# A two-block transformer kernel: bias rows made in the context's tail, a third buffer for modulation weights, and shift and scale columns turned on TensorE from SBUF

## The chip, the cores and the metric

The kernel runs on one core of a Trainium2 chip. The metric is device time in microseconds (us), the median of several executions; the profile is of one execution of its own.

## What is computed

Two blocks run one after the other on 256 tokens of width 1024. The first (two layers) is a hybrid mixer (retention, a block attention whose scores get a relative bias from a small table, a short convolution) and a convolutional feed-forward part. The second (two layers) attends from the tokens to themselves and to a context of 256 tokens, and ends each layer in a PEER mixture: every token picks 128 of 16384 experts, and for each pick a row `u` and a row `v` of 1024 values are fetched. Shift, scale and gate of every norm come from a condition vector by the modulation matrices:

```python
for l in range(DEPTH):
    last = l == DEPTH - 1
    sh1, s1, g1, sh2, s2, g2 = jnp.split((sc @ w_mod[l] + b_mod[l])[:, None, :], 6, axis=-1)
    csh1, cs1, cg1, csh2, cs2, cg2 = jnp.split(sc_ctx @ w_mod[l] + b_mod[l], 6, axis=-1)
    hc = modulate(h_ctx, csh1, cs1)
    ...
def modulate(x, shift, scale):
    return rms(x) * (1 + scale) + shift
...
    b_own = rel_t[:, t5_bucket(dist_own)]
    s_own = jnp.einsum('bhqd,bhld->bhql', qi, k_own) * scale + b_own[None]
```

The context's own path (norm, modulation, projection, attention, PEER) doesn't depend on the first block, so the kernel does it first.

## The kernel before, in words

There are three parts, one after the other on every engine: the context (the second block's first layer on the context tokens), the first block ("first", two layers), and the latent part (the second block on the tokens, two layers). Each engine runs its own instruction list, in the order in which the code is written; semaphores tie them together. All direct loads are issued by SyncE (SP) in its order, a few by ScalarE (ACT); the fetches of expert rows (128 rows of 4 KB each) are issued by GpSimd (POOL). The fetches of the context's PEER run beside the first block: ten row buffers, eight in `ROWS` and two in `ACC`, each fetched again when VectorE (DVE) has used it (`beside_used`).

**Modulations.** There are twelve, g = 0 to 11, six for each layer; each is a product of two columns with a 1024x1024 matrix of 4 MiB, 64 matmul records and 8 for the bias row (`mod_pe`, L445 and L448), a copy by ScalarE (`mod_act`, L459) and two stores to `mod_dram`. g = 0 and 1 (shift and scale of the context's first norm) are wanted first; 2 to 5 stand inside the context's projections and mixer; 6 to 11 behind its PEER queries. The matrices of g = 3 to 11 go by turns into the lower half (slots 0, 1) and the upper half (slots 2, 3) of the weight buffer `W`; those of 0 to 2 go in four pieces of 1 MiB into other buffers. One row `MODB` holds the bias of the next modulation.

**Setup.** TensorE makes six rows of relative bias over distance (L1636), ScalarE stores them to `rel_dram` (L1674), and twelve loads issued by ScalarE (L1682) bring them back as overlapping windows `HANK`. TensorE does modulation 0, waits for all twelve, reverses them by six products with `flip` (L1644), and then does modulation 1. ScalarE stores the six bias tiles to `bias_dram`, and brings shift and scale back from `mod_dram` as 16 rows `MODR` (`mod_rows`, L347), which TensorE turns into columns `MODC` (L543). ScalarE applies them while it copies the turned context into `XT` (L928); then the projections start (L322).

**The tail of the context.** While DVE searches the best experts of both token tiles, the loads and products of modulations 6 to 11 run. SyncE's order there is: load g after modulation g - 2 (for g = 7: after the last queries, which read slots 2 and 3), bias row g after modulation g - 1. Behind the last come the first weights of the first block and its input `X`.

**The handover.** The semaphores of the first block's first layer were used by the setup, so GpSimd clears them (`clear_layer(pool, 0)`) and raises `cleared`; TensorE, SyncE, ScalarE and DVE wait for it before the first block. In the kernel before, GpSimd does this in the middle of the context's mixer.

Of the kernel before, what the change touches and what calls it, by code (L numbers as in the profile page):

```python
# [23 lines left out]
ALU = mybir.AluOpType  # L24
# [3 lines left out]
P = 128  # L28
# [68 lines left out]
MOD_SETUP, MOD_FIRST = 2, 3  # L97
# [85 lines left out]
def program(nc, A, out):  # L183
    with ExitStack() as ctx:
# [21 lines left out]
        act_step = sem("act_step")  # L206
        mod_read = sem("mod_read")
        mod_loaded = [sem(f"mod_loaded{i}") for i in range(2)]
# [199 lines left out]

        def mod_piece(g, j):

            if g < MOD_FIRST:
                return PIECES[min(g, 1)][j].rearrange("p (k n) -> p k n", k=DK)
            half = W[:, 2 * (g % 2):2 * (g % 2) + 2, :].rearrange("p s n -> p (s n)").rearrange("p (j k n) -> p j k n", j=MODP, k=DK)
            return half[:, j]
# [4 lines left out]
        def mod_landed(g):  # L419
            return mod_loaded[1 if g == MOD_SETUP else g % 2]  # L420

        def mod_load(sp, g):
            l, i = divmod(g, MODS_N)
            n = P * D * D // P
            src = A["w_mod_2"][l, i * n:(i + 1) * n].rearrange("(p j k n) -> p j k n", p=P, j=MODP, k=DK)
            if g < MOD_FIRST:
                for j in range(MODP):
                    sp.dma_start(mod_piece(g, j), src[:, j]).then_inc(mod_landed(g), 16)
            else:
                half = W[:, 2 * (g % 2):2 * (g % 2) + 2, :].rearrange("p s n -> p (s n)").rearrange("p (j k n) -> p j k n", j=MODP, k=DK)  # L430
                sp.dma_start(half, src).then_inc(mod_landed(g), 16)
# [5 lines left out]
        def mod_pe(pe, s, banks, groups, g):  # L437
            pe.wait_ge(mod_landed(g), 16 * sum(MODP if i < MOD_FIRST else 1 for i in range(g + 1) if mod_landed(i) is mod_landed(g)))
# [98 lines left out]
        def stream_pe_cols(pe, s, banks, groups, stage):  # L537

            pe.wait_ge(small_loaded, 16 * 5 * (stage + 1))
# [1066 lines left out]
        with ExitStack() as ph:  # L1606
# [6 lines left out]
            PIECES = [[AR[:, 0:2 * D], AR[:, 2 * D:4 * D], AR[:, 4 * D:6 * D], BC["QKT"][:]], [AR[:, 6 * D:8 * D], HF, KV[:], ACCF]]  # L1613
            QRF, VF, EIF = (BC[name][:].rearrange("p t n -> p (t n)") for name in ("QR", "V", "EI"))
# [6 lines left out]
            HANK = [BC["PROJ2"][:, h * NB:(h + 1) * NB] for h in range(4)] + [QRF[:, h * NB:(h + 1) * NB] for h in range(2)]  # L1621
# [84 lines left out]
            def context_pe(pe):  # L1706
# [13 lines left out]
                for g in range(MOD_FIRST + 3, L * MODS_N):  # L1720
                    mod_pe(pe, s, banks, groups, g)
# [1167 lines left out]
```

## Time and profile before

| | |
|---|---|
| median of 3 runs | 3053.81 us (3052.48 to 3056.08) |
| profiled execution: its time, its span | 3025.97 us, 3024.2 us |
| mean granted TensorE clock, share of full | 0.897 |
| TensorE, VectorE, ScalarE, GpSimd busy | 2483.7, 2114.5, 831.5, 1115.7 us |
| moved by DMA | 1038.89 MB, mean 344 GB/s |
| chain of waits: DMA, VectorE, TensorE | 31%, 29%, 26% |

Busy shares are means over stages with different limits; the chain of waits tells which one ends last at each moment. The profiled execution took 27.8 us less than the median of the runs.

### The profile page before, as it was taken

To read this page: it belongs to the slowest core of one execution; us is meant where nothing else is said; L and a number is where in the kernel's file an instruction comes from. 1 tells how busy PE (TensorE), PEld (TensorE's weight loads), DVE (VectorE), ACT (ScalarE), POOL (GpSimd) and SP (SyncE) were. 2 spreads that over 40 slices of the span, in tenths; PEclk is the share of its full clock that TensorE was granted. 3 is DMA by queue.
4 is the path that set the end of the run, shared out by engine and by line. 5 is a ranking of instruction groups with operands and counts; after the bars stand their busy time and mean duration, and the time that the engine had idled before them with its cause. 6 is when DMAs were issued, how large, how long until landed. Compare 5 with 4: busy or idle time off the path is not lost.

```text
span 3024.2 us, 27795 instructions
## 1 busy us (share of the span) xinstructions
PE 2483.7 (82%) x8607; PEld 1401.7 (46%) x8607; DVE 2114.5 (70%) x4458; ACT 831.5 (27%) x2284; POOL 1115.7 (37%) x1121
## 2 busy tenths in 40 slices
PE   2997698878898899889788778778798798778776
PEld 1655355655546566555444333323365344333322
DVE  0359769878788988777587677755374776777654
ACT  1131111100012100023443333334324343433343
POOL 0200245666553676460133334333210333333332
PEclk7898796999997999987999889989998899898999
DMA  8255999999999999970499899999830999999998
GB/s 323 112 195 232 388 415 361 384 410 408 403 396 369 398 409 413 390 288 6 173 402 413 360 420 419 417 413 396 329 116 4 366 418 366 420 420 416 418 420 337
DMA packets 182646, 1038.89 MB, mean 344 GB/s; under 512 B 26891, under 2 KB 28914, under 8 KB 99812
## 3 DMA queue, kind: packets, MB, share of 16 engines
q0 software_dynamic: 147456, 805.37, 66.1%
q1 hardware_dynamic: 32700, 229.20, 18.9%
q10 hardware_dynamic: 2344, 2.55, 0.2%
q8 instruction: 70, 1.15, 0.2%
q14 instruction: 76, 0.62, 0.1%
HBM read 1032.61 MB, written 4.44 MB: 343 GB/s over the span
## 4 chain that ended last, share of the span: by engine, by line
DMA 31%; DVE 29%; PE 26%; issue 6%; POOL 4%; ACT 4%; ACTq 0%; SPq 0%; DVEq 0%; POOLq 0%
DMA W<-in_peer_uv,IDX 14%; PE PS L2581 12%; DMA ROWS<-in_peer_uv,IDX 7%; PE PS L322 7%; DVE ROWS L1326 3%; DMA ROWS<-in_peer_uv,COEF 3%; DVE ROWS L2212 3%; POOL ROWS L2412 3%; DVE W L2712 2%; DMA ROWS<-in_peer_uv,IDXV 2%; DVE PROD L2225 2%; PE PS L2013 1%; DVE BJ L1523 1%; DMA G<-in_peer_uv,IDX 1%; PE PS L2023 1%
## 5 line engine op out<-in xcount | busy, mean ns | idle before, releaser
L2581 PE MATMUL PS<-W,SCALE 128*128 128x512 f32 x1712 | 841.5, 639 | 220.7 <-ACT SCALE L2665 220.2
L2712 DVE CUSTOM_DVE_ANT_0 W<-W,PS 128x1024 f32<-128x1024 f32 x428 | 515.2, 1219 | 331.6 <-DMA W<-in_peer_uv,IDX 330.3
L2765 POOL DMA_INDIRECT W<-in_peer_uv,IDX x428 | 407.8, 953 | 687.9 <-PE PS L2581 668.6
L2581 PEld LDWEIGHTS PS<-W,SCALE 128*128 128x128 f32 x1712 | 331.2, 203 | 707.8 <-issue 706.2
L2412 POOL DMA_INDIRECT ROWS<-in_peer_uv,IDX x206 | 216.4, 1050 | 396.2 <-DVE IDX L1587 201.0
L2013 PE MATMUL PS<-XT,W 128*128 128x256 f32 x1408 | 307.8, 380 | 0.0
L2013 PEld LDWEIGHTS PS<-XT,W 128*128 128x128 f32 x1408 | 268.4, 191 | 46.1 <-issue 10.7
L2658 ACT ACTIVATE DOT<-DOT 128x1 f32<-128x1 f32 x512 | 103.6, 202 | 652.7 <-DVE DOT L2712 646.3
L322 PE MATMUL PS<-W,XT 128*128 128x512 f32 (+2 forms) x576 | 220.6, 545 | 10.7 <-ACT XT L928 5.7
L322 PE MATMUL PS<-XT,W 128*128 128x128 f32 (+1 forms) x1344 | 215.4, 320 | 5.7 <-ACT XT L1039 5.7
L2665 ACT ACTIVATE SCALE<-C,COEF 128x128 f32<-128x128 f32 x512 | 205.6, 402 | 48.1 <-PE PS L2581 1.5
L2212 DVE CUSTOM_DVE_ANT_0 ROWS<-ROWS,PS 128x1024 f32<-128x1024 f32 x154 | 182.4, 1216 | 47.3 <-DMA ROWS<-in_peer_uv,IDX 45.5
L322 PEld LDWEIGHTS PS<-XT,W 128*128 128x128 f32 x1344 | 198.0, 191 | 28.5 <-issue 6.7
L322 PEld LDWEIGHTS PS<-W,XT 128*128 128x128 f32 x576 | 108.9, 199 | 120.0 <-issue 108.9
L2661 ACT ACTIVATE COEF<-DOT,WGT 128x1 f32<-128x1 f32 x512 | 150.8, 295 | 48.3 <-ACT DOT L2658 0.7
L322 PE MATMUL PS<-W,CT 128*128 128x512 f32 x320 | 150.2, 629 | 5.2 <-ACT CT L1090 2.5
L2225 DVE SCALAR_TENSOR_TENSOR PROD<-ROWS,COEF,PROD 128x1024 f32<-128x1024 f32 x102 | 131.0, 1284 | 31.4 <-DMA ROWS<-in_peer_uv,COEF 22.2
L2412 POOL DMA_INDIRECT ROWS<-in_peer_uv,COEF x102 | 112.1, 1099 | 57.2 <-DVE PROD L2225 30.9
L2225 DVE SCALAR_TENSOR_TENSOR H<-ROWS,COEF,H 128x1024 f32<-128x1024 f32 x81 | 104.0, 1284 | 27.8 <-DMA ROWS<-in_peer_uv,IDXV 21.5
L2023 PE MATMUL PS<-W,PP 128*128 128x512 f32 x192 | 94.2, 648 | 27.8 <-DVE PP L2380 27.8
L2412 POOL DMA_INDIRECT ROWS<-in_peer_uv,IDXV x82 | 96.1, 1172 | 55.9 <-DVE H L2225 35.8
L1326 DVE SCALAR_TENSOR_TENSOR ROWS<-ROWS,COLC 128x256 f32<-128x256 f32 x270 | 115.1, 481 | 2.3
(386 smaller groups left out, 3141.9 us busy)
## 6 DMA issues: line engine op xcount, KB each, us to landing
W<-in_w_up SPq DMA_DIRECT2D x44, 1024.0 KB, 11.9
W<-in_w_in SPq DMA_DIRECT2D x21, 2048.0 KB, 11.3
W<-in_w_mod SPq DMA_DIRECT2D x9, 4096.0 KB, 14.4
W<-in_w_down SPq DMA_DIRECT2D x22, 1024.0 KB, 8.0
W<-in_w_o SPq DMA_DIRECT2D x6, 2048.0 KB, 9.5
W<-in_peer_wq SPq DMA_DIRECT2D x6, 2048.0 KB, 10.9
W<-in_w_out SPq DMA_DIRECT2D x4, 2048.0 KB, 12.4
W<-in_peer_uv,IDX POOLq DMA_INDIRECT x428, 12.8
```

Of the source, the lines that this page charges most:

```text
L322: ins = nc.tensor.matmul(PS[:, b, cols[0]:cols[1]], lhs(k), rhs(k), start=start and k == 0, stop=stop and k == n_k - 1)
L1326: ins = nc.vector.scalar_tensor_tensor(B["U"][:, j, :], B["PAD"][:, j, k:k + S], tap, B["U"][:, j, :], ALU.mult, ALU.add)
L2013: ins = nc.tensor.matmul(PS[:, 2 * r + half, j * S:(j + 1) * S], up_half(i, half)[:, k, j * P:(j + 1) * P], XT[:, k, :], start=(k == 0), s ...
L2023: ins = nc.tensor.matmul(PS[:, 4 + 2 * t + n, :], HG[r][:, j, t * P:(t + 1) * P], wslot(2 + r, 2, D)[:, j, n * 512:(n + 1) * 512], start=F ...
L2212: nc.vector.tensor_tensor_reduce(beside_slot(l, m), beside_slot(l, m), h, 1.0, 0.0, ALU.mult, ALU.add, DOT[:, 0, m:m + 1]).then_inc(beside ...
L2225: nc.vector.scalar_tensor_tensor(total, slot, coef, total, ALU.mult, ALU.add).then_inc(beside_used, 1)
L2412: nc.gpsimd.indirect_dma_start(beside_slot(l, n), None, one_by_one, bass.IndirectOffsetOnAxis(index[:, n % PICKS:n % PICKS + 1], 0),).then ...
L2581: ins = nc.tensor.matmul(PS[:, SUMS2[t] + h, :], SCALE[:, n % NSCALE, :], v_of(n)[:, h * 512:(h + 1) * 512], start=m == 0, stop=m == PICKS ...
L2661: nc.scalar.activation(COEF[:, t, one], DOT[:, t, one], ACT.Copy, scale=WGT[:, t, one]).then_inc(s.coef_ready, 1)
L2665: nc.scalar.activation(SCALE[:, n % NSCALE, :], ident, ACT.Copy, scale=COEF[:, t, one]).then_inc(s.scale_ready, 1)
L2712: nc.vector.tensor_tensor_reduce(u_of(n), u_of(n), h_of(t), 1.0, 0.0, ALU.mult, ALU.add, DOT[:, t, m:m + 1]).then_inc(s.rows_used, 1)
L2765: nc.gpsimd.indirect_dma_start(pair_slot(n), None, in_pairs, bass.IndirectOffsetOnAxis(IDX[:, t, m:m + 1], 0),).then_inc(pair_landed[fetch ...
```

## The change

- The twelve loads of the bias windows, the six products with `flip` and the stores to `bias_dram` move from the setup into the tail, behind modulation 7. SyncE issues the loads; the windows and the bias tiles lie in `ROWS` and `V`.
- Shift and scale of the context's first norm: TensorE turns `MODS` (the copy of modulations 0 and 1 in SBUF) by four transposes, and DVE takes the wanted columns from PSUM; the way through `mod_dram` stays for the rows that are wanted later.
- Modulation buffers: a third home `TAIL` (the buffers `CT`, `QKT`, `ACC`, `XT`) for g = 7 and 10; modulation 2 gets a semaphore of its own. Loads are issued one modulation earlier relative to their use.
- `clear_layer(pool, 0)` moves from the context's mixer to GpSimd's place between the fetch of row 9 and that of row 10, and waits for `X`.

```diff
+MOD_SETUP, MOD_BESIDE = 2, 6
+FRONT, SECOND, LOWER, UPPER, TAIL = range(5)
+MOD_HOME = [FRONT, SECOND, SECOND, UPPER, LOWER, UPPER, LOWER, TAIL, UPPER, LOWER, TAIL, UPPER]
...
+            PIECES = {FRONT: [AR[:, 0:2 * D], AR[:, 2 * D:4 * D], AR[:, 4 * D:6 * D], BC["QKT"][:]],
+                      SECOND: [AR[:, 6 * D:8 * D], HF, KV[:], ACCF], TAIL: [CTF, BC["QKT"][:], ACCF, XTF]}
...
                 pe.wait_ge(s.cols_ready, 1)
-                mod_pe(pe, s, banks, groups, 0)
+                for g in range(MOD_SETUP):
+                    mod_pe(pe, s, banks, groups, g)
+
+            def bias_pe(pe, banks):
+                s, groups = layers[0], of_setup
                 pe.wait_ge(s.late_rows_loaded, 12 * 16)
                 for h in range(MOBA_H):
                     b = banks.take(s.score_read, h + 1)
                     nc.tensor.matmul(PS[:, b, 0:NB], flip, HANK[h], start=True, stop=True).then_inc(s.groups_done, groups.mark("bias", h))
                     groups.at["bias", h, "bank"] = b
-                mod_pe(pe, s, banks, groups, 1)
...
+            def context_pe_cols(pe, banks):
+                s, groups = layers[1], of_context
+                pe.wait_ge(small_loaded, 16 * 4)
+                b = banks.take(s.cols_ready, 1)
+                for j in range(CW2 // P):
+                    ins = nc.tensor.transpose(PS[:, b, j * 34:j * 34 + 34], COLR[:, j * P:(j + 1) * P], ident[0:34, 0:34])
+                ins.then_inc(s.groups_done, groups.mark("cols"))
+                groups.at["cols", "bank"] = b
+                b = banks.take(s.cols_ready, 1)
+                for g in range(MOD_SETUP):
+                    pe.wait_ge(mod_read, g + 1)
+                    for half in range(2):
+                        o = (2 * g + half) * P
+                        ins = nc.tensor.transpose(PS[:, b, o:o + P], MODS[:, g, half * P:(half + 1) * P], ident)
+                ins.then_inc(s.groups_done, groups.mark("modT"))
...
                 stream_sp(sp, s, groups, BC, 0, 1, beside, first=1)
                 sp.wait_ge(s.groups_done, groups.of("mix", 1, TT - 1))
-                mod_load(sp, MOD_FIRST + 3)
+                mod_load(sp, 6)
+                for j in range(2):
+                    mod_load_piece(sp, 7, j)
...
+                sp.wait_ge(s.h_ready, TT)
+                mod_load_piece(sp, 7, 2)
+                sp.wait_ge(s.groups_done, groups.of("pq", TT - 1, 1))
+                mod_load_piece(sp, 7, 3)
+                mod_load(sp, 8)
+                sp.wait_ge(s.groups_done, groups.of("ps", TT - 1, 1, 1))
+                sp.wait_ge(layers[0].stored, 16)
+                bias_sp(sp)
+                for g in range(7, L * MODS_N):
                     sp.wait_ge(s.groups_done, groups.of("mod", g - 1))
                     mod_bias(sp, g)
-                for c in (0, 1):
-                    first_load(sp, c, 0)
+                    if g + 2 < L * MODS_N:
+                        mod_load(sp, g + 2)
+                    elif g + 2 == L * MODS_N:
+                        for c in (0, 1):
+                            first_load(sp, c, 0)
+                sp.wait_ge(layers[0].stored, 3 * 16)
...
-                pool.wait_ge(s.probs_ready, 1)
-                pool.wait_ge(s.max_ready, 1)
-                pool.wait_ge(s.weights_loaded[2], 16)
-                clear_layer(pool, 0)
...
+                        if l == 0 and n == 6:
+                            pool.wait_ge(layers[0].stored, 3 * 16)
+                        if l == 0 and n == RING:
+                            pool.wait_ge(layers[1].groups_done, of_context.of("mod", 10))
+                        if l == 0 and n == BESIDE:
+                            pool.wait_ge(x_loaded, 16)
+                            clear_layer(pool, 0)
```

How the instructions stand shows what the diff alone leaves open. First ScalarE's list in the setup before, from its copy of the bias over distance (`V`) to the first activation that makes `XT`; `mod_dram<-X` are the stores of a modulation.

```order
L1674 DMA rel_dram<-V 6x511 [waits act_step]
...
L1682 DMA QR<-rel_dram 128x256
L459 COPY X<-PS 128x256 [waits groups_done_0]
L463 DMA mod_dram<-X 4x256 [waits mod_read]
L463 DMA mod_dram<-X 4x256
L1686 COPY QKT<-PS 128x384 [waits groups_done_0] x5
L1686 COPY QR<-PS 128x384 [waits groups_done_0]
L459 COPY X<-PS 128x256 [waits groups_done_0]
...
L347 DMA G<-mod_dram 16x128 [waits mod_stored1,mod_stored0]
L1691 DMA bias_dram<-QKT 128x1920 [waits score_read_0]
L1692 DMA bias_dram<-QR 128x384
L928 ACTIVATE XT<-PS,MODC 128x128 [waits groups_done_1,cols_ready_1]
```

Twelve loads, six copies, the load of `MODR` and two stores stand between modulation 0's place and the first activation there. In the changed kernel the same stretch of TensorE's list, from the bias row of modulation 1 (`ROW`) to the first projection, reads as follows; `G` holds the small rows, `X` is `MODS`.

```order
L456 MATMUL PS<-ROW,ONE 32x256 x4
L561 MATMUL PS<-C,CT 128x128 [waits norm_ready_1]
L561 MATMUL PS<-C,CT 128x128 x7
L561 MATMUL PS<-C,CT 128x128 [waits cols_ready_0,norm_ready_1]
L561 MATMUL PS<-C,CT 128x128 x3
L561 MATMUL PS<-C,CT 128x128 [waits proj_ready_0]
L561 MATMUL PS<-C,CT 128x128 x3
L1725 MATMUL PS<-C,G 128x34 [waits mod_read,small_loaded]
L1725 MATMUL PS<-C,G 128x34 x3
L1733 MATMUL PS<-C,X 128x128 [waits mod_read]
...
L323 MATMUL PS<-W,XT 128x512 [waits xT_ready_1,first_loaded0]
```

The sixteen transposes of the context stand behind modulation 1 in both kernels; what follows them now waits for ScalarE's copy of modulation 1 alone. Last, GpSimd's list of the changed kernel from the first fetch to row 10; the `ISA` row is the clearing, `x_loaded` the load of `X` behind all modulations.

```order
L2471 DMA ROWS<-in_peer_uv,IDX 128x1024 [waits picks_ready_1]
L2471 DMA ROWS<-in_peer_uv,IDX 128x1024
L2471 DMA ROWS<-in_peer_uv,IDX 128x1024 [waits picks_ready_1]
L2471 DMA ROWS<-in_peer_uv,IDX 128x1024 x3
L2471 DMA ROWS<-in_peer_uv,IDX 128x1024 [waits stored_0]
L2471 DMA ROWS<-in_peer_uv,IDX 128x1024
L2471 DMA ACC<-in_peer_uv,IDX 128x1024 [waits groups_done_1]
L2471 DMA ACC<-in_peer_uv,IDX 128x1024
L233 ISA [waits x_loaded]
L2471 DMA ROWS<-in_peer_uv,IDX 128x1024 [waits beside_used] x8
```

In the kernel before, the clearing stands ahead of all these fetches and waits for the context's mixer only.

## Rows read from the trace of the kernel before

**Rows 1.** The page: mean busy share of 16 DMA engines, 40 slices, in tenths.

```profile
DMA  8255999999999999970499899999830999999998
```

**Rows 2.** Chain of waits, setup to projections: start us, length us, what.

```profile
21.30 27.27 DMA QR<-rel_dram
...
55.75 3.59 PE PS L445 x64
...
60.90 5.07 DMA mod_dram<-X
66.05 5.71 DMA G<-mod_dram
...
73.18 2.91 ACT XT L928 x8
76.13 13.49 PE PS L322 x32
89.64 38.21 PE PS L322 x160
```

**Rows 3.** Chain of waits, first block's start.

```profile
352.55 22.22 DMA ROWS<-in_peer_uv,IDX
...
438.02 21.24 DMA ROWS<-in_peer_uv,IDX
...
471.50 0.88 DVE NM L2278
```

**Rows 4.** SyncE's issues at 6 to 31 us, and KB each, us to landing.

```profile
6.86 0.43 SPq L428 DMA_DIRECT2D ACC<-in_w_mod  x1
...
27.38 3.82 SPq L343 DMA_DIRECT2D W<-in_w_in  x4
...
ACC<-in_w_mod SPq DMA_DIRECT2D x1, 1024.0 KB, 24.4
...
G<-in_q_gain SPq DMA_DIRECT2D x1, 32.0 KB, 12.0
...
W<-in_w_in SPq DMA_DIRECT2D x1, 2048.0 KB, 15.9
```

**Rows 5.** ScalarE's DMA queue at 11.5:31.3, 31.3:52: packets, MB, share of engines.

```profile
q10 hardware_dynamic: 1089, 0.74, 13.1%
...
q10 hardware_dynamic: 655, 0.45, 6.9%
```

**Rows 6.** Timeline, TensorE: turns after modulation 1, and modulation 11.

```profile
59.84 1.97 PE L553 MATMUL PS<-C,CT 128*128 128x128 f32 x16
...
330.14 5.83 PE L445 MATMUL PS<-W,DOT 128*32 128x256 f32 x64 [4.17 <-DMA W<-in_w_mod]
335.90 0.63 PE L448 MATMUL PS<-X,ONE 1*32 1x256 f32 x8
```

**Rows 7.** Windows: us, busy of PE, PEld, DVE, ACT, POOL, PEclk, DMA, GB/s.

```profile
275.00:335.00 60.00, 34.65 (x388) 15.24 (x384) 58.52 (x233) 1.86 (x5) 2.08 (x2) 0.66 0.97 403
```

**Rows 8.** SyncE's issue behind modulation 11, and landing of X in us.

```profile
339.33 0.31 SPq L365 DMA_DIRECT2D RAW<-in_ffn_conv_w  x1
...
X<-in_x SPq DMA_DIRECT2D x1, 1024.0 KB, 5.0
```

**Rows 9.** Timeline at the handover: DVE's last index, row 9, TensorE's start.

```profile
340.81 0.22 DVE L1587 TENSOR_SCALAR IDX<-EI 128x128 int32<-128x128 f32 x1
...
350.07 0.94 POOL L2412 DMA_INDIRECT ACC<-in_peer_uv,IDX  x1 [0.31 <-issue]
...
345.25 0.35 PE L1886 MATMUL PS<-C,RAW 72*128 72x72 f32 x1 [8.71 <-DMA X<-in_x]
```

**Rows 10.** Timeline: the 42nd row, DVE's first retention product, TensorE's before it.

```profile
436.52 1.22 DVE L2212 CUSTOM_DVE_ANT_0 ROWS<-ROWS,PS 128x1024 f32<-128x1024 f32 x1 [3.11 <-DMA ROWS<-in_peer_uv,IDX]
...
453.92 0.55 DVE L2265 TENSOR_TENSOR PP<-PS,DEC 128x384 f32<-128x384 f32 x1
...
449.61 0.71 PE L1930 MATMUL PS<-XT 64*128 64x256 f32 x4 [1.37 <-ACT XT L2152]
```

More of the change, by code:

```diff
@@ L205, in program @@
         consts_loaded = sem("consts_loaded")
-        act_step = sem("act_step")
         mod_read = sem("mod_read")
-        mod_loaded = [sem(f"mod_loaded{i}") for i in range(2)]
+        mod_loaded = [sem(f"mod_loaded{i}") for i in range(3)]
         mod_bias_loaded = sem("mod_bias_loaded")
@@ L1645, in setup_pe, with bias_sp, bias_act @@
                     groups.at["bias", h, "bank"] = b
-                mod_pe(pe, s, banks, groups, 1)
+            def bias_sp(sp):
+                for h in range(MOBA_H):
+                    for first, n, o in ((P, P, 0), (0, 2 * P, P)):
+                        src = bass.AP(rel_dram, h * (2 * S - 1) + first, [[1, P], [1, n]])
+                        sp.dma_start(HANK[h][:, o:o + n], src).then_inc(layers[0].late_rows_loaded, 16)
+            def bias_act(act):
+                s, groups = layers[0], of_setup
+                for h in range(MOBA_H):
+                    act.wait_ge(s.groups_done, groups.of("bias", h))
+                    nc.scalar.copy(HANK[h], PS[:, groups.at["bias", h, "bank"], 0:NB]).then_inc(s.score_read, 1)
+                act.wait_ge(s.score_read, MOBA_H)
+                act.dma_start(bias_dram[:, 0:5 * NB], AR[:, 6 * D:6 * D + 5 * NB]).then_inc(s.stored, 16)
+                act.dma_start(bias_dram[:, 5 * NB:6 * NB], HANK[5]).then_inc(s.stored, 16)
             def setup_sp(sp):
@@ L1711, in context_pe @@
                     stream_pe_turn(pe, s, banks, groups, BC, t)
[L1712 removed]
+                context_pe_cols(pe, banks)
                 def beside(banks, i):
@@ L1718, in context_pe @@
                 context_mixer_pe(pe, s, banks, groups, BC, beside)
-                for g in range(MOD_FIRST + 3, L * MODS_N):
+                for g in range(MOD_BESIDE, L * MODS_N):
                     mod_pe(pe, s, banks, groups, g)
+                    if g == BIAS_BEHIND:
+                        bias_pe(pe, banks)
             def context_sp(sp):
@@ L1776, in context_act @@
                 context_mixer_act(act, s, groups, BC, beside)
-                for g in range(MOD_FIRST + 3, L * MODS_N):
+                for g in range(MOD_BESIDE, L * MODS_N):
                     mod_act(act, s, groups, g)
+                    if g == BIAS_BEHIND:
+                        bias_act(act)
                 for t in range(TT):
```

106 lines of the change are left out of this document (51 added, 55 removed).

## The prediction

> **What bounds the kernel now.** I read the page first. From the fifth slice on nearly every digit of the DMA row is a 9 [rows 1]: behind the context the kernel lives on the rows that it fetches, with two or three holes. Ahead of that stands the context, in which the DMA engines are half idle, so an order of work must bound it. I therefore went to the chain of waits. In the setup it is one wait after the other [rows 2]: the twelve bias windows until 48.6 us (21.30 + 27.27), their six products, modulation 1 from 55.75, then shift and scale out to DRAM (60.90, 5.07 us) and back (66.05, 5.71 us), ScalarE's copy (73.18, 2.91 us), and only at 76.13 the first projection. From there TensorE works for 51.7 us without a hole (13.49 + 38.21), and DVE's searches carry the chain to the last index at 340.81 [rows 9]. Behind it come the row fetches: the chain lies on their landings [rows 3] until the 42nd row at 436.5 [rows 10], and on DVE from 471 on.
>
> So two places can matter: the 76.1 us ahead of the projections, and the handover at 341 to 352 us, through which all later work is shifted as a whole. All times below are in the clock of the kernel before; what the setup saves is taken off once, at the end.
>
> **1. The setup.** What ends last now, once the windows are gone? Modulation 1's matrix: its last piece was issued at 6.86 and landed 24.4 us later [rows 4], at 31.3. In the stretch from 11.5 to 31.3 us, 13.1% of the DMA engines' time went to ScalarE's queue, which is the bias windows [rows 5]: 0.131 x 19.8 = 2.6 us. The piece lands at 28.7 without them. Modulation 1 then takes between 4.1 us (55.75 to 59.84, TensorE busy just before [rows 2, 6]) and 6.4 us (330.14 to 336.53, TensorE idle just before [rows 6]). TensorE ends modulation 0 shortly before, so I lean to the middle: 5.2, end at 33.9. Behind it stand the sixteen turns of the context, 1.97 us [rows 6]; the four column transposes and the four new ones, each no longer than one of these sixteen (0.12 us), so about 1.0 with ScalarE's copy hidden behind the turns; DVE's three small operations, bounded by the 1.4 us between the load of `MODR` (71.77) and ScalarE's start at 73.18 [rows 2], of which I take 0.9; ScalarE's 2.9 us. Sum: 33.9 + 2.0 + 1.0 + 0.9 + 2.9 = 40.7.
>
> The projection also needs its first weights. They were issued at 27.38 and landed 15.9 us later [rows 4], at 43.3. The windows' queue took 2.6 us before 31.3 and 6.9% of the 12 us after [rows 5], 0.8 us: 39.9 without it. So the projections start at 40.7, and the setup saves 76.1 - 40.7 = **35.4 us**. Bounds: 36.2 (weights bind, modulation 1 in 4.1), and 31 if piece and weights land as before (43.3, and columns at 45). The weights of the later chunks are behind these in the queue, but are wanted 20 us later.
>
> Between the projections and the last index nothing is added to DVE's list, and TensorE gets nothing between its queries. Modulation 3's load is issued before modulation 2 instead of behind it, and the pieces of modulation 7 fill a hole at 245 to 270 us; neither is on the chain. I cost both at nothing.
>
> **2. The tail.** What the third buffer gives is eaten by where the bias row stands. Bias row g is now issued behind load g + 1 (of which it used to be ahead), so modulation g starts only when load g + 1 has landed. That a small load waits for those issued before it is in the trace: `q_gain`, 32 KB, took 12.0 us to land in the setup [rows 4], behind the pieces of modulation 1. From the last queries at 271.7 the queue carries until bias row 11: a piece and load 8 (1.05 + 4.19 MB), the windows (1.18), loads 9 to 11 (12.58), the stores to `bias_dram` (1.18) and two chunks of the first block (4.19): 24.4 MB. At the 403 GB/s of this stretch [rows 7] that is 60.5 us, to which I add 1.5 us for the first landing and 2 for the windows' small packets: 335.7. Modulation 11 at 6.4 us [rows 6] ends at 342.1, against 336.5 before. From its end to SyncE's next issue were 2.8 us (336.53 to 339.33), X is the third issue, 0.7 later, and lands in 5.0 [rows 6, 8]: X is there at 350.6, against 345.0 before.
>
> The Trainium skill puts it otherwise ("DMA: Bandwidth & Descriptors", Specifications): a core's share of HBM is about 358 GB/s. By that the 24.4 MB take 68 us and all of this ends 7.6 us later. The trace has 403 over these 60 us [rows 7], and that is what I use.
>
> **3. The handover.** The clearing now stands behind row 9 on GpSimd and waits for X. Row 9 was issued at 350.07 + 0.94 = 351.0 [rows 9], ten microseconds behind the last index, since each fetch costs GpSimd 1.24 us; so `cleared` rises at about 351.2, bound by GpSimd with X 0.6 us ahead. Four engines wait for it. Queued behind: TensorE's 345.25 [rows 9] becomes 351.5, **6.3 us** later; SyncE's tables and weights; ScalarE's copy; DVE's first product, and with that row 10.
>
> How much of it stays? The DMA engines don't go idle: eight fetches are issued one each 1.24 us, 0.52 MB each, which alone is 420 GB/s. So the 42nd row comes at 436.5 plus at most 2 us (what X and weights moved in the hole before 343 us). TensorE, 6.3 us late and never idle until then, gives the first retention product at 450.1 + 6.3 + 0.4 = 456.9 where DVE took it at 453.92 [rows 10]. The chain is 3.0 us late from there. Bounds: 0 if DVE finds other work, 6.3 if all stays.
>
> **Sum.** -35.4 + 3.0 = -32.4 us. Against its own time: 3025.97 - 32.4 = 2993.6. The runs' median lies 27.8 above the profiled execution; I know no term of the change that depends on it, so 3053.8 - 32.4 = **3021.4 us**. Within 0.2%, about 6 us, this measurement couldn't be told from no change.
>
> **The rivals.**
> - *The handover is free.* The fetches stay full and the chain lies on them [rows 3]; 3053.8 - 35.4 = 3018.4. Against it: DVE follows TensorE from 450 on. Chance 0.2.
> - *The tail is late.* Modulation 11 ends later than 342: SyncE stands while it issues twelve small loads behind 5 MB, or the rate falls. X then decides, not GpSimd. With the rate that makes the tail 7.6 us longer, X lands at 358.2, TensorE starts 13.4 late, the chain is 10 late: 3028.4; at 15 us longer, 3036. Speaks for it: those loads took 27 us in the setup [rows 2]. Against: there they shared with 15 MB. Chance 0.2, of which a quarter for a lower rate. The Trainium skill's 358 GB/s ("DMA: Bandwidth & Descriptors", Specifications) would end here.
> - *The setup saves less.* Piece and weights are bound by the total of bytes, not by the windows' queue: start at 45, 31 saved, 3025.8. Chance 0.12.
> - *The change doesn't show.* Less than 6 us is left if the handover costs 29: X at 377 or so. Chance 0.03: 3051.
> - *Slower.* The same wait decides alone: `cleared` hangs on X, X on bias row 11. The first 3.3 us of TensorE's delay are free (6.3 cost 3.0), each further one counts in full, so the sign turns when TensorE starts 38.7 us late: X at 383.7, 33 us behind the forecast, for which the tail's 24.4 MB must run at 260 GB/s. With the tail 40 us longer TensorE is 45.6 late, the chain 42.3: 3060.7. Nothing in the rows supports it; chance 0.02.
>
> **Numbers.** The forecast has 0.43, its own range 3017 to 3027. Faster by over 0.2%: 0.43 + 0.2 + 0.2 + 0.12 = 0.95; same 0.03; slower 0.02. For eight in ten the range takes in the free handover with the best setup (36.2 saved: 3017.6, less 3 for the run to run spread) and the late tail up to 15 us: 3014 to 3037.
>
> **What the changed profile would show.** First projection at 40 to 42 us, with the wait before it on ScalarE's `XT`, not on a DMA; last index near 305.4. In the tail, modulations 8 to 11 released by a DMA and the gap between them 10 to 11 us; modulation 11 ends at 306.7. `cleared` by the wait of TensorE's first transpose, released by GpSimd at 316; DMA share at least 0.95 from 310 to 440. The prediction is wrong if X lands after row 9's issue by more than 3 us, if the first weights come after 43, or if DVE waits for TensorE more than 4 us ahead of the retention.

## The result, and the profile of the changed kernel

The changed kernel takes 3027.6 us (median of 15 runs, 3021.15 to 3049.2), the kernel before 3051.5 in the same measurement (15 runs, 3038.4 to 3057.1): ratio 0.9934, 95% interval 0.9917 to 0.9951. By the ratio that is 20 us less (15 to 25), by the medians 24. On another chip the same pair later gave 2999.1 against 3026.0, ratio 0.9912 (0.9893 to 0.9931), 27 us less. The prediction had 32.4 us less. The mean of the two ratios, 0.9923, is 23.5 us less; it stands for the changed kernel below. So the prediction had the sign and most of the gain, and some 9 of its 32 us are missing.

The profiled execution took 3021.15 us (span 3019.3), only 4.8 less than before's own 3025.97. That small difference misleads; the last section shows why.

The page's DMA row, which answers to [rows 1]:

```profile
DMA  8458998999988999970499999999830998999998
```

The fifth slice (302 to 377 us) is a 9, and in the stretch from 310 to 440 us the share is 1.00, as forecast. New are the 8s of the twelfth and thirteenth slice (830 to 981 us), both 9 before; the last section comes to them. The seventh slice (453 to 528 us) is an 8 too, where it was a 9; no run looked into that.

**The setup** came out as worked out. Chain of waits, changed kernel (start us, length us, what), which answers to [rows 2]:

```profile
6.91 21.78 DMA ACC<-in_w_mod
...
28.73 5.35 PE PS L453 x64
34.07 0.56 PE PS L456 x8
34.64 1.90 PE PS L561 x16
...
38.01 2.91 ACT XT L936 x8
...
40.96 13.48 PE PS L323 x32
...
54.47 38.21 PE PS L323 x160
```

The windows and the trip through DRAM are gone. The projections start at 40.96 us instead of 76.13: 35.2 us earlier. They wait for ScalarE, as forecast. DVE writes the last index at 305.63 instead of 340.81 [rows 9], and those are still 35.2 us: nothing between the two places ate any of it.

**The tail and the handover** did not. Four views of the changed kernel. First the timeline of SyncE (start us, length us, line, what, count), in the context's tail:

```profile
238.37 12.24 SPq L1665 DMA_DIRECT2D ROWS<-rel_dram  x10
250.65 2.28 SPq L1665 DMA_DIRECT2D V<-rel_dram  x2
252.98 0.29 SPq L443 DMA_DIRECT2D X<-in_b_mod  x1
...
298.35 0.24 SPq L443 DMA_DIRECT2D X<-in_b_mod  x1
317.07 0.31 SPq L366 DMA_DIRECT2D RAW<-in_ffn_conv_w  x1
```

Then the timeline of TensorE: modulations 7 and 11, modulation 11's bias product, and the first block's first instruction:

```profile
256.98 0.61 PE L453 MATMUL PS<-CT,DOT 128*32 128x256 f32 x1 [14.53 <-issue]
...
302.42 5.35 PE L453 MATMUL PS<-W,DOT 128*32 128x256 f32 x64 [4.13 <-issue]
307.70 0.63 PE L456 MATMUL PS<-X,ONE 1*32 1x256 f32 x8
```

The chain of waits behind it:

```profile
310.31 0.38 ACT X L467
...
311.23 5.75 DMA mod_dram<-X
...
317.76 6.93 DMA X<-in_x
...
324.72 0.34 POOLq L233
...
325.11 0.38 PE PS L1938
...
327.87 16.80 PE PS L323 x32
...
345.54 79.24 PE PS L323 x256
```

And GpSimd's timeline: rows 2 and 9:

```profile
306.13 0.94 POOL L2471 DMA_INDIRECT ROWS<-in_peer_uv,IDX  x1 [45.87 <-DVE IDX L1595]
...
314.82 0.99 POOL L2471 DMA_INDIRECT ACC<-in_peer_uv,IDX  x1 [0.30 <-issue]
```

What to see: SyncE stands 14.5 us in twelve small loads, so bias row 7 goes out at 252.98 and modulation 7 waits 14.5 us. Modulation 11 leaves TensorE at 308.33 all the same, close to the 306.7 of the prediction. From there it gets worse. ScalarE's copy comes 2.0 us later, the store takes until 317.0, and X needs 6.93 us. X lands at 324.69, 8.9 us behind the issue of row 9 (315.81), where the prediction had it 0.6 us ahead. TensorE's first block starts at 325.11 instead of 345.25 [rows 9]: 20.1 us earlier and not 29. And the chain in the first block lies on TensorE now (97 us of matmuls), no longer on the row fetches [rows 3].

### The profile page after: what moved, and what is told of

Its sections match the earlier page's. It is cut to its first block, busy times and chain, and to the rows that moved or that the text cites. A ratio compares the mean times of both kernels' runs of the same rounds, so it can differ in the third digit from the quotient of the medians.

```text
span 3019.3 us, 27807 instructions
## 1 busy us (share of the span) xinstructions
PE 2482.1 (82%) x8610; PEld 1400.3 (46%) x8610; DVE 2113.8 (70%) x4458; ACT 830.6 (28%) x2284; POOL 1120.1 (37%) x1121
## 3 DMA queue, kind: packets, MB, share of 16 engines
q1 hardware_dynamic: 35292, 230.38, 19.2%
## 4 chain that ended last, share of the span: by engine, by line
PE 35%; DMA 25%; DVE 24%; issue 7%; POOL 5%; ACT 4%; another core or an unknown queue 0%; SPq 0%; ACTq 0%; DVEq 0%; POOLq 0%
PE PS L323 14%; DMA W<-in_peer_uv,IDX 14%; PE PS L2640 12%; DMA ROWS<-in_peer_uv,COEF 3%; DMA ROWS<-in_peer_uv,IDXV 3%; DVE ROWS L1334 3%; POOL ROWS L2471 3%; DVE ROWS L2264 2%; DVE W L2771 2%; DMA ROWS<-in_peer_uv,IDX 2%; PE PS L2065 2%; PE PS L2075 1%; PE PS L453 1%; DMA G<-in_peer_uv,IDX 1%; DVE PROD L2277 1%
## 5 line engine op out<-in xcount | busy, mean ns | idle before, releaser
L323 PE MATMUL PS<-W,XT 128*128 128x512 f32 (+2 forms) x576 | 229.7, 557 | 23.9 <-issue 16.8
## 6 DMA issues: line engine op xcount, KB each, us to landing
W<-in_w_out SPq DMA_DIRECT2D x4, 2048.0 KB, 10.2
```

The source lines that it names most:

```text
L323: ins = nc.tensor.matmul(PS[:, b, cols[0]:cols[1]], lhs(k), rhs(k), start=start and k == 0, stop=stop and k == n_k - 1)
```

## The experiments

All times are of the profiled execution, ratios against the kernel before on the same chip. "Start" is TensorE's first instruction of the first block, "retention" DVE's first retention product [rows 10].

| kernel | last index | start | start less index | retention | ratio (95% interval) |
|---|---|---|---|---|---|
| before | 340.81 | 345.25 | 4.4 | 453.92 | 1 |
| before_again | 338.19 | 342.12 | 3.9 | 449.58 | |
| changed | 305.63 | 325.11 | 19.5 | 431.51 | 0.9934 (0.9917 to 0.9951) |
| after_again | 306.23 | 325.44 | 19.2 | 432.02 | 0.9912 (0.9893 to 0.9931) |
| two_buffers | 304.26 | 324.43 | 20.2 | 430.52 | 0.9946 (0.9927 to 0.9964) |
| bias_ahead | 306.80 | 315.35 | 8.6 | 420.44 | 0.9896 (0.9877 to 0.9916) |
| windows_act | 306.69 | 331.31 | 24.6 | 436.87 | 0.9963 (0.9946 to 0.9980) |
| cols_dram | 315.86 | 337.78 | 21.9 | 444.19 | 0.9978 (0.9960 to 0.9995) |
| x_split | 306.31 | 327.97 | 21.7 | 434.61 | 0.9916 (0.9893 to 0.9940) |
| ahead_split | 304.34 | 311.23 | 6.9 | 416.71 | 0.9902 (0.9875 to 0.9928) |
| bias_setup | 329.58 | 333.04 | 3.5 | 440.28 | 0.9965 (0.9948 to 0.9983) |
| windows_later | 310.10 | 330.05 | 20.0 | 435.96 | 0.9927 (0.9901 to 0.9953) |
| fetch_late | 305.69 | 317.07 | 11.4 | 425.53 | 0.9927 (0.9904 to 0.9951) |
| all_three | 310.90 | 313.46 | 2.6 | 419.51 | 0.9892 (0.9866 to 0.9918) |

An interval is 5 to 8 us wide to each side, and the difference of two ratios is less certain than either: a ratio alone tells two kernels apart from some 8 us on. Where less matters I go by the times in the profile, and there by the distance from the last index. The last index itself differs by up to 7 us between kernels whose setup is the same, for reasons that lie ahead of the tail: from modulation 6's first product to it are 67.4 us in every trace. In windows_later and all_three it is 4.5 and 5.3 us late; TensorE's granted clock was lower there in the context's mixer (0.50 and 0.54 at 160 to 170 us, 0.69 in the changed kernel).

**What the two parts of the setup are worth: cols_dram and bias_setup.** cols_dram takes the columns back through DRAM:

```diff
-                context_pe_cols(pe, banks)
+                stream_pe_cols(pe, s, banks, groups, 0)
...
+                mod_stored_to(act, MOD_SETUP - 1)
+                mod_rows(act, 0, 1)
```

> Changed kernel with one of its parts undone: shift and scale columns of the context go through DRAM again (store, load of MODR by ScalarE's queue, four transposes of 34 rows), the bias windows stay in the tail. From before's chain store and load took 5.07 + 5.71 us and four gaps; the projections then start at 40.96 + 11 = 51 to 53 us instead of 40.96. If the setup's gain reaches the end in full, as the prediction has it, the time is 10 to 12 us above the changed kernel's: 3038 to 3040. Rival: half of it or less, since something else behind the context (row fetches, TensorE's rate) sets the end: 3028 to 3033.

Chain of waits, cols_dram:

```profile
35.57 6.03 DMA mod_dram<-X
...
41.68 5.24 DMA G<-mod_dram
...
48.33 2.92 ACT XT L936 x8
...
51.29 3.78 PE PS L323 x4
```

The projections start 10.3 us later, the last index 10.2, the first block 12.7, and the ratio is 17 us above that of the changed kernel (0.0055 x 3055, with some 7 us to each side). The retention comes 12.7 us later. So what the setup saves reaches the end, and the forecast of 10 to 12 us lies within the interval. No run looks into the 2.4 us that the start loses beyond the last index.

bias_setup takes the windows and their products back into the setup, on ScalarE's queue, and out of the tail:

```diff
-                for g in range(MOD_SETUP):
-                    mod_pe(pe, s, banks, groups, g)
+                mod_pe(pe, s, banks, groups, 0)
+                bias_pe(pe, banks)
+                mod_pe(pe, s, banks, groups, 1)
...
-                    if g == BIAS_BEHIND:
-                        bias_pe(pe, banks)
```

> Changed kernel with its other part undone: the twelve bias windows and their products go back into the setup on ScalarE's queue, between modulations 0 and 1, and out of the tail; columns are still turned from SBUF, three buffers and the order of bias rows stay. By before's chain modulation 1 then ends at 59.8 to 60.9 us and the projections start at 64 to 66 instead of 40.96, 23 to 25 us later. The tail loses SyncE's 14.5 us in small loads, so behind the last index (329 to 331) X is no later than in before relative to it: theory A/C, that the tail and not the last index sets the start of the first block, gives TensorE's start at 335 to 342, that is 10 to 17 us later than the changed kernel, 3038 to 3045. If windows in the tail cost nothing: 23 to 25 us later in all, 3050 to 3053.

Chain of waits, bias_setup:

```profile
21.60 27.65 DMA QR<-rel_dram
...
62.67 2.91 ACT XT L936 x8
...
65.63 4.54 PE PS L323 x6
```

The projections start 24.7 us later and the last index 24.0. But the first block starts only 7.9 us later than in the changed kernel, less than the 10 to 17 us expected, and the ratio is 13 us up (0.0042 x 3048, with some 7 us to each side). So moving the windows saves 24 us ahead of the last index and gives 16 back behind it. From last index to start are 3.5 us here (4.4 before) and 19.5 in the changed kernel. Half of the 16 us lie in the tail: from modulation 6's first product to modulation 11's end are 62.2 us here, 63.1 before and 70.1 in the changed kernel. The other half lies behind modulation 11.

**Where the 16 us go: bias rows, buffers, windows.** two_buffers:

```diff
-MOD_HOME = [..., LOWER, TAIL, UPPER, LOWER, TAIL, UPPER]
+MOD_HOME = [..., LOWER, UPPER, LOWER, UPPER, LOWER, UPPER]
...
                     mod_bias(sp, g)
-                    if g + 2 < L * MODS_N:
-                        mod_load(sp, g + 2)
...
+                    if g + 1 < L * MODS_N:
+                        mod_load(sp, g + 1)
```

> Changed kernel, but modulation 7 goes back to the upper half of W, so the tail has two buffers again and load g+1 is issued behind bias row g once modulation g-1 is done; the first block's chunks 0 and 1 are issued behind bias row 11. Theory A (the tail is late because a bias row stands behind a load that it doesn't need): modulation 11's copy comes at 300 to 305 us instead of 310.3, X lands by 316 instead of 324.7, TensorE's first block starts at 316 to 317 (bound by GpSimd's row 9) instead of 325, and the time is 7 to 9 us below the changed kernel's: 3019 to 3021, 0.990 of the kernel before. Theory B (the third buffer earns what the bias row takes; the tail is bound by bytes and by SyncE's small loads): the copy comes at 310 or later, the time is 3027 to 3035.

Modulation 11's copy comes at 307.60, between the two theories; the start at 324.43 (325.11) and the ratio are the changed kernel's (X is issued 3.3 us earlier, but takes 9.5 us instead of 6.9). From modulation 6's first product to modulation 11's end are 69.6 us, 70.1 in the changed kernel. So Theory B comes nearer: what the third buffer gives, the bias row behind the load takes. bias_ahead keeps the third buffer and parts the two:

```diff
-            return BC["ROW"][2][0:1, :] if g == MOD_SETUP - 1 else MODB
+            return BC["ROW"][2][0:1, :] if g in (MOD_SETUP - 1, 8, 10) else MODB
...
                     sp.wait_ge(s.groups_done, groups.of("mod", g - 1))
-                    mod_bias(sp, g)
+                    if g == 7:
+                        mod_bias(sp, g)
+                    if g + 1 < L * MODS_N:
+                        mod_bias(sp, g + 1)
```

> Changed kernel with three buffers and a second place for the bias row (rows 8 and 10 in ROW), so that bias row g+1 is issued ahead of load g+2 and only behind its own load; own semaphore for the even ones. Theory A (bias rows behind loads): the waits of modulations 9 and 10 on a DMA shrink to what the loads need, the copy of modulation 11 comes at 298 to 303 us, X lands at 312 to 316, TensorE's first block starts at 316 to 317, 3019 to 3021. Theory B (bytes and SyncE's stand of 14.5 us bound it): modulation 11's copy stays within 3 us of 310.3, and the time is that of the changed kernel, 3025 to 3030.

TensorE's timeline, bias_ahead:

```profile
297.21 5.33 PE L457 MATMUL PS<-W,DOT 128*32 128x256 f32 x64 [4.10 <-DMA W<-in_w_mod]
302.47 0.63 PE L460 MATMUL PS<-X,ONE 1*32 1x256 f32 x8
315.35 0.38 PE L1945 MATMUL PS<-C,RAW 72*128 72x72 f32 x1 [12.25 <-DMA X<-in_x]
```

Modulation 11 waits for its own matrix and for nothing else. It ends 5.2 us earlier, its copy comes 7.1 us earlier, X lands at 315.0 and not 324.7, and the block starts 9.8 us earlier (10.9 counted from the last index). The ratio falls to 0.9896, 8 us below the changed kernel's (0.0027 x 3055, with some 7 us to each side); the two later kernels that keep this edit, ahead_split and all_three, have 0.9902 and 0.9892. Theory A holds here: the bias row is what makes modulation 11 late, once there is a buffer to use the time.

The windows' place, twice. windows_act lets ScalarE's queue issue them, windows_later puts them behind bias row 7 and load 9:

```diff
-                bias_sp(sp)
...
                 context_mixer_act(act, s, groups, BC, beside)
...
+                bias_in(act)
```

> Changed kernel with the twelve bias windows issued by ScalarE's queue instead of SyncE's; bias rows still behind loads. Theory C (SyncE's 14.5 us in the small loads, from 238.4 to 252.9 us, make the tail late): bias row 7 is issued at 243 instead of 253, modulation 7 starts 8 to 10 us earlier (247 to 249), everything behind it too, X lands by 316, the time is 3019 to 3021. Theory A alone (bias rows behind loads): modulation 7 starts earlier, but modulation 11 ends within 4 us of 310.3 since the bytes ahead of bias row 11 are the same; 3023 to 3028.

```diff
-                bias_sp(sp)
                 for g in range(7, L * MODS_N):
...
+                    if g == 7:
...
+                        bias_sp(sp)
```

> Changed kernel with the twelve bias windows still issued by SyncE, but behind bias row 7 and load 9 instead of ahead of them, and their products behind modulation 9 instead of 7. Theory C (SyncE's stand in the small loads costs the tail its start): bias row 7 is issued at 243 instead of 253 and modulation 7 starts at 245 to 248 instead of 257; modulation 11 ends on TensorE at 298 to 303 instead of 308.3, X lands 5 to 9 us earlier, the time is 5 to 9 us below the changed kernel's (ratio 0.990 to 0.992). Rival: the tail is bound by its 24 MB; modulation 11 ends within 3 us of 308.3, ratio 0.9925 to 0.995.

Timelines: ScalarE and TensorE of windows_act, then SyncE of windows_later:

```profile
249.47 9.81 ACTq L1665 DMA_DIRECT2D ROWS<-rel_dram  x1
259.31 5.27 ACTq L1665 DMA_DIRECT2D V<-rel_dram  x2
...
280.00 5.18 PE L1658 MATMUL PS<-ROWS,C 128*128 128x384 f32 x10 [19.16 <-DMA V<-rel_dram]
```

```profile
247.71 18.41 SPq L1665 DMA_DIRECT2D ROWS<-rel_dram  x10
266.16 2.05 SPq L1665 DMA_DIRECT2D V<-rel_dram  x2
268.25 0.37 SPq L443 DMA_DIRECT2D X<-in_b_mod  x1
```

Both misses. ScalarE stands as long as SyncE did (15.1 us against 14.5), the windows land at 280, TensorE waits 19 us for them and the block starts 6.2 us later (12 us slower by the ratio). The Trainium skill has the reason in general ("SBUF — State Buffer", "Can I just issue two DMAs to hit both halves?"): all DMAs of a kernel land on the same 16 engines, and issuing from several engines doesn't help; the trace agrees. In windows_later bias row 7 goes out 6 us earlier (247.00), yet modulation 7 starts at 256.20 and not before: the row stands behind load 8. Behind another 4 MB load the windows cost SyncE 20.5 us instead of 14.5, and bias row 8 is now late too (268.25). From last index to start are 20.0 us, as in the changed kernel (19.5). Theory C, that a better place for the windows mends the tail, is refuted for both places. That the windows cost the tail nothing isn't shown by that, and bias_setup says otherwise: without them the tail is 7.9 us shorter (62.2 against 70.1), of which bias_ahead gets 6.4 back (63.7) with the windows in place.

**What happens behind modulation 11: x_split, fetch_late.** x_split loads tile 0 of X as soon as modulation 11 is done:

```diff
+                sp.dma_start(X[:, 0, :], x_dram[:, 0, :]).then_inc(x_loaded, 16)
+                raw_load(sp, 0)
                 mod_stored_to(sp, L * MODS_N - 1)
-                raw_load(sp, 0)
-                sp.dma_start(X[:], x_dram).then_inc(x_loaded, 16)
+                sp.dma_start(X[:, 1, :], x_dram[:, 1, :]).then_inc(x_loaded, 16)
```

> Changed kernel with X loaded in two halves: token tile 0 (whose row 0 held the bias row) as soon as modulation 11 is done, tile 1 behind the stores of the modulation as before. Theory A' (the last 14 us ahead of the first block are one wait after the other: copy 310.3, store 5.75, X 6.93): tile 1 is half as large and is issued at 317.8 or a little later, so X lands 2 to 4 us earlier, TensorE starts at 321 to 323, the time is 2 to 4 us less: 3024 to 3026. Rival: the half's landing is bound by the queue of row fetches ahead of it, not by its size; no change, within 1 us at TensorE's start.

Timeline of ScalarE, x_split:

```profile
318.22 0.37 ACT L467 COPY X<-PS 128x256 f32<-128x256 f32 x1 [17.20 <-remote]
```

Not what I had expected. Modulation 11 left TensorE at 311.8, but ScalarE copied it 6.4 us later. It waits for two things there, and TensorE was done; the other is a store. The copy goes to the half of `MODS` from which modulation 9 is stored, and that small store, issued at 291, was not back. The halves help (the second takes 4.0 us instead of 6.9), the store undoes it: start 327.97. The same wait is 2.0 us in the changed kernel, 6.7 in cols_dram, and none in bias_ahead, where modulation 9 is stored 10 us earlier (278.2 instead of 288.8).

fetch_late holds GpSimd's rows until modulation 11 is stored and clears in front of row 6:

```diff
+                        if l == 0 and n == 2:
+                            pool.wait_ge(layers[1].groups_done, of_context.of("mod", L * MODS_N - 1))
+                            mod_stored_to(pool, L * MODS_N - 1)
                         if l == 0 and n == 6:
                             pool.wait_ge(layers[0].stored, 3 * 16)
+                            pool.wait_ge(x_loaded, 16)
+                            clear_layer(pool, 0)
```

> Changed kernel, but GpSimd's row fetches from the third on wait until modulation 11 is stored, and `cleared` rises before row 6. Theory E (the end of the tail is stretched by the row fetches that now share the DMA engines: the store took 5.8 instead of 2.3 us and X 6.9 instead of 5.0, since 4 MB of rows are issued ahead of them from 306 us on): store back in 2 to 3 us, X issued at 314 and landed at 319 to 320 instead of 324.7, TensorE starts 5 us earlier; the rows come 7 us later. If TensorE's start sets the end, as the changed kernel's chain has it (TensorE 325 to 420 us), the time falls by 3 to 5 us, ratio 0.992; if the row fetches set it, as the prediction had it, the time rises by 5 to 8 us, ratio 0.995 to 0.996.

Windows of the changed kernel and of fetch_late (us, busy of PE, PEld, DVE, ACT, POOL, then PEclk, DMA share, GB/s), and from the issues of fetch_late how many us X took:

```profile
316.00:325.00 9.00, 0.00 (x0) 0.00 (x0) 0.00 (x0) 0.00 (x0) 0.00 (x0) 0.50 1.05 410
```

```profile
306.00:312.00 6.00, 2.33 (x40) 0.90 (x31) 0.60 (x3) 2.16 (x4) 0.32 (x1) 0.97 0.01 4
312.00:318.00 6.00, 0.93 (x5) 0.94 (x6) 1.44 (x6) 0.95 (x1) 3.69 (x5) 0.59 0.89 332
```

```profile
X<-in_x SPq DMA_DIRECT2D x1, 1024.0 KB, 4.9
```

In the changed kernel all engines stand for 9 us while the DMA engines run full, with rows that nobody can use yet ahead of the X that everybody waits for. Without the rows the store is back 2.6 us after the copy (6.8 in the changed kernel), X needs 4.9 instead of 6.9, and TensorE starts 8.0 us earlier. The other kernels that load X whole agree. Where the copy falls among the issues of the rows (the changed kernel twice, two_buffers, windows_later), SyncE goes on 6.2 to 6.8 us after it, elsewhere after 2.6 to 4.3; X takes 6.8 to 9.5 us where a row was issued within 3 us ahead of it, and 4.8 to 5.0 elsewhere. Half of theory E holds. But the DMA engines idle at 306 to 312 us, DVE then waits 35 us for rows from 326 to 470 us (18.5 in the changed kernel; before, up to 490 us, 40), and the retention gains 6.0 of the 8.0. The ratio, 0.9927, can't be told from the changed kernel's. So in the first block both lines lie close: TensorE's when X is late, the rows' when they are.

**Together: ahead_split and all_three.**

> bias_ahead and x_split together. In bias_ahead TensorE's first transposes waited for X, landed at 315.3, with GpSimd's row 9 about as late. So theory: X comes 2 to 3 us earlier but `cleared` is then bound by GpSimd's row 9 at 315 to 316, TensorE starts within 1 us of 315.35, and the time is bias_ahead's within 3 us (ratio 0.988 to 0.991). Rival: GpSimd isn't the bound; TensorE starts at 312 to 313, 0.986 to 0.988.

> The changed kernel with bias rows ahead, windows behind load 9, and X in two halves. With each cause of the late tail gone, modulation 11 ends on TensorE at 290 to 296, X is issued and landed before or at the last index (303 to 306), and TensorE's first block is bound by `cleared` behind GpSimd's row 9 at 315 to 316, or by X at 305 to 311. The first gives 10 us less than the changed kernel (0.990), as bias_ahead; the second 14 to 18 us less (0.988). If neither the start of the first block nor X matter any more, it is the same as bias_ahead (0.9896).

ahead_split (bias_ahead and x_split) starts at 311.23, released by X, all_three (windows_later too) at 313.46, with a last index that itself is 5 us late there. Timelines of ahead_split, TensorE's start and GpSimd's row 9:

```profile
311.23 0.38 PE L1946 MATMUL PS<-C,RAW 72*128 72x72 f32 x1 [11.36 <-DMA X<-in_x]
...
313.62 0.94 POOL L2479 DMA_INDIRECT ACC<-in_peer_uv,IDX  x1 [0.30 <-issue]
```

This refutes the expectation (its rival holds for the start), and with it a step of the prediction: GpSimd's row 9 does not hold back `cleared`. The clearing stands behind row 9 in GpSimd's list, yet the profile has it at 310.8 us, as soon as X is there and 2.8 us before row 9's own record begins. In bias_setup it comes at 332.7, 6.1 us before row 9 (338.84), in all_three at 313.1, 7.1 us before it (320.17), in bias_ahead at 315.0, 1.0 us before it. In each of them, and in the changed kernel (324.7), it follows the landing of X. So in these traces GpSimd's list goes on while its fetches are still being made up, one each 1.24 us, and X alone sets the start. all_three misses its expectation in the tail as well: modulation 11 is copied at 303.58, not at 290 to 296.

Their ratios, 0.9902 and 0.9892, are bias_ahead's. With the bias row in its own place X is near the last index again (start less index 8.6, 6.9 and 2.6 us), and nothing more is gained at the end within what the measurement can tell. The version to keep is bias_ahead, about 1% below the kernel before.

**The profiles themselves: before_again, after_again.**

> The kernel before, unchanged, once more with a profile. What is asked is TensorE's slow stretch: in the changed kernel, and in all four experiments so far, TensorE issues only 4 to 9 matmuls in 10 us instead of 25 for 25 to 30 us in the second layer's first block (856 to 886 us in the changed kernel), with the granted clock at 0.5 to 0.8, and in the profiled execution of before it doesn't. Theory D: the stretch is a state of the chip that before also meets in nearly all its runs (their median lies 25 to 28 us above the profiled one); then this execution shows it between 865 and 925 us and its time is 3045 to 3057. Rival: only the changed order of work brings it about; then it isn't here, the time is 3025 to 3030 in this execution, and the 25 us are a cost of the change that its saving pays for.

> The changed kernel, unchanged, with a second profile. Theory: its tail and handover repeat (modulation 11 off TensorE at 307 to 310, the copy behind it held up to 310 or later by modulation 9's store, X landed 9 to 12 us behind GpSimd's row 9, TensorE's first block from 325 to 328), ratio 0.992 to 0.995; TensorE's slow stretch at 855 to 885 us, if this chip has it, adds 25 us to it and to before alike, so the ratio stays and only the times move. Rival: the tail differs by more than 4 us from run to run and the experiments' differences of that size say nothing.

The tail repeats within 0.4 us at the start of the block, but not by the same path: modulation 9's store held the copy by nothing in the second profile, against the expectation, and by 2.0 in the first, and X took 8.5 us instead of 6.9. The ratio, 0.9912, is a little better than expected. before_again took 3042.26 us, where 3045 to 3057 were expected. TensorE's slow stretch has the last section.

## Why the prediction was right, and which steps of it were not

- **The setup, 35.4 us: measured 35.2.** Each term stood: piece at 28.7 (28.69), modulation 1 in 5.2 (5.9), turns and transposes 3.0 (2.9), DVE 0.9 (0.5), ScalarE 2.9 (2.9), start 40.7 (40.96). cols_dram shows that it carries to the end.
- **The tail, bias row 11 at 335.7 in before's clock, modulation 11's end at 342.1.** Less 35.4 that is 300.3 and 306.7; measured 302.4 and 308.33. The order behind the bias row was read rightly, and bias_ahead shows it by undoing it. That SyncE stands in the windows was in the rival "the tail is late", and it happened (14.5 us); against the forecast modulation 11 is only these 1.6 us late. The DMA engines had work all the same: from 236 to 302 us their share is 0.98, at 384 GB/s instead of the 403 reckoned.
- **The step that was mis-sized: "from its end to SyncE's next issue were 2.8 us ..., X is the third issue, 0.7 later, and lands in 5.0".** These are prices from before, where the last index comes 4.2 us behind modulation 11's copy and the store runs with no row fetch beside it. In the changed kernel the last index lies ahead of the copy, and from 306 us GpSimd issues eight rows of 0.52 MB into the same DMA engines. Measured: 2.0 until the copy (modulation 9's store), 6.8 until SyncE's issue, 0.7, and X in 6.93. X lands at 324.69 and not 315.2. The 9.5 us are 1.6 of modulation 11, 5.9 of the stores, 1.9 of X. fetch_late shows the last two with and without the rows; of the 5.9 us, the 2.0 ahead of the copy didn't repeat in after_again. I had counted each of the eight fetches for GpSimd's time, and none of them as traffic ahead of X.
- **The step that was wrong: "`cleared` rises at about 351.2, bound by GpSimd with X 0.6 us ahead".** The rise is bound by X alone: in ahead_split it comes 2.8 us before row 9's record begins, in bias_setup 6.1. That this did not show in the forecast is luck: X was reckoned 0.6 us ahead of the clearing, so the wrong bound moved the start by less than 1 us.
- **The handover: TensorE 6.3 us late, the chain 3.0.** TensorE starts 9.0 us behind the predicted 316.1, and DVE takes the retention product at 431.51. 453.92 - 35.2 is 418.7, so the chain is 12.8 us late: the 3.0 and further 9.8. The rule that beyond 3.3 us "each further one counts in full" holds within a microsecond.
- **The sum.** -35.2 + 12.8 = -22.4 us at the retention; measured at the end -20 and -27 by the ratios. The measured 3027.6 lies in the wide range (3014 to 3037) and just outside the forecast's own (3017 to 3027). Two of the three signs that I gave for being wrong were there: X lands 8.9 us after row 9's issue (the limit was 3), and ahead of the retention DVE stands for 8.0, 8.3 and 2.4 us before products that need TensorE's results (the limit was 4). What came is half of the rival "the tail is late": X is late, by 9.5 us, between that rival's two cases, but not through modulation 11, which was to be the reason. The chance of 0.2 that I gave it was too low; what I missed is that a tail which ends behind the last index is stretched by the very fetches that the last index lets go.

## What to carry to other kernels

When an edit brings two stages closer together, durations taken from the old trace no longer hold at the seam: ask which transfers of the next stage are issued ahead of the last transfers of this one, and price these with the queue that they will then find. A small load that gates an engine belongs ahead of the large load that it doesn't need; here a second row of 4 KB gave about a third of what the whole change had (8 us, with some 7 to each side, of 23.5). A place in an engine's list is not a time: the clearing behind ten fetches came up to 7 us before the last of them was made up. And before a difference of two profiled executions is believed, lay their landmarks side by side: a gain of 23 us was all there at 817 us and gone at 906, for a reason that had nothing to do with the edit.

## What the hardware showed that I had not expected

**TensorE slows down by itself in one place, on some chips.** In the second layer's first block TensorE multiplies 512-column tiles for some 50 us without a hole. Windows of 10 us (columns as above): the changed kernel, then before_again, then after_again in the same place:

```profile
866.00:876.00 10.00, 6.06 (x8) 1.66 (x7) 7.79 (x13) 0.00 (x0) 7.47 (x8) 0.67 1.02 409
876.00:886.00 10.00, 7.33 (x9) 2.58 (x9) 0.81 (x2) 1.75 (x3) 2.83 (x4) 0.50 1.03 409
...
896.00:906.00 10.00, 10.00 (x25) 4.47 (x24) 0.00 (x0) 0.59 (x1) 0.00 (x0) 1.00 0.04 15
```

```profile
882.00:892.00 10.00, 5.92 (x7) 1.73 (x7) 5.56 (x10) 0.00 (x0) 5.64 (x6) 0.50 1.00 410
892.00:902.00 10.00, 7.27 (x9) 2.30 (x9) 6.82 (x12) 0.16 (x1) 7.52 (x8) 0.67 1.03 410
```

```profile
866.00:876.00 10.00, 10.00 (x25) 4.42 (x24) 7.20 (x13) 1.17 (x2) 5.72 (x7) 1.00 1.02 413
```

6 to 9 matmuls in 10 us instead of 25, for about 30 us, with the granted clock between its full 2.4 GHz and the half, after 45 us of unbroken work at full clock. (At 345 to 420 us of the same execution TensorE works 75 us without a hole at full clock and doesn't slow down.) A halved clock alone would leave 12: at the start of the first block, at granted clock 0.5, the same 512-column matmuls come 0.85 us apart, 0.40 at full clock. In the stretch they have holes of up to 2.9 us between them, and the profile shows nothing that TensorE waits for in these. TensorE then holds up DVE and GpSimd until the DMA engines run dry (0.04 at 896 us). It costs some 25 us, as SyncE's timelines show when they are laid side by side, first before's, then the changed kernel's:

```profile
839.74 0.33 SPq L2107 DMA_DIRECT2D cs_dram<-PROD  x1
...
904.67 3.90 SPq L2049 DMA_DIRECT2D W<-in_w_out  x2
```

```profile
816.63 0.33 SPq L2159 DMA_DIRECT2D cs_dram<-PROD  x1
...
906.09 3.90 SPq L2101 DMA_DIRECT2D W<-in_w_out  x2
```

The changed kernel goes into that block 23 us ahead of before's profile and comes out 1.4 us behind. The stretch is in the changed kernel's first profile and in all eight later ones that were taken on two chips (before_again among them), where the kernel before takes 3048 and 3055 us; it is in none of the four on two other chips, where it takes 3023 and 3026. Before's first profile (3025.97) doesn't have it either, its runs (3052 to 3056) lie where executions with it lie. So it belongs to the chip or the execution and not to the change, and with its some 25 us it is the likely source of the 27.8 us between profile and median that the prediction couldn't explain (before_again, which has it, took 3042.26). What sets it off is open: no run here varied TensorE's load in that place.

**A small store takes long in traffic.** Modulation 9's 4 KB stores, issued at 288.8 us, were back at 310.3, 21.5 us later, with 8 MB of loads and the first rows in flight (27 us in x_split and cols_dram; under 20 in after_again, where they held up nothing); modulation 11's in before took 2.3. The Trainium skill says ("DMA: Bandwidth & Descriptors", "HWDGE ordering") that a DMA engine's semaphore increment lands only after all its earlier writes, those of other queues too. That would make such a store wait for loads that it has nothing to do with. No run here isolates it.
